# One transpose and one product per differential step, four buffers for squares, and convolution taps turned by TensorE

## What is computed

```python
# differential attention: two softmax maps of one head, subtracted
sc = einsum('bqhcd,bkhcd->bchqk', qb, k) * scale + bias
p = softmax(where(dist >= 0, sc, -inf), axis=-1)
w = p[:, 0] - lam * p[:, 1]
out = einsum('bhqk,bkhd->bqhd', w, v)          # then rmsnorm over each head's 128 values

# feed-forward: a causal convolution of three taps per channel, then a gate
u = causal_dwconv(h @ ffn_up, ffn_conv_w, ffn_conv_b)
u_gate, u_val = split(u, 2)
x = x + (gelu(u_gate) * u_val) @ ffn_down

# SSD mixer: chunk by chunk, at its end a norm over each group of 512 channels
return grouped_rms_norm(y * silu(z), norm_w, SSD_GROUPS)
```

## Time and profile before

| | |
|---|---|
| median of 3 runs | 3296.1 us (3293.46 to 3296.81) |
| the profiled execution's own time | 3299.9 us |
| its span, first to last instruction | 3298.2 us |
| TensorE matmuls busy | 3095.4 us, 94% |
| VectorE, ScalarE, GpSimd busy | 43%, 34%, 23% |
| mean granted TensorE clock | 0.972 of full speed |

### The profile page before, as it was taken

One profiled execution on the slowest core, in us unless ns is written; L12 is line 12 of the kernel. 1 busy time (PEld: TensorE's weight loads), 2 busy tenths in 40 slices (PEclk: granted clock), 3 DMA queues, 4 the chain that ended last, 5 costly groups with the idle time before them and its releaser, 6 DMA issues. The chain is left out here.

```text
span 3298.2 us, 39762 instructions
## 1 busy us (share of the span) xinstructions
PE 3095.4 (94%) x15115; PEld 2529.9 (77%) x15115; DVE 1422.1 (43%) x2254; ACT 1120.1 (34%) x1462; POOL 746.5 (23%) x482
## 2 busy tenths in 40 slices
PE   8998899989999999989999999978798999999988
PEld 6676777777877788868888888857777888878766
DVE  4345223411134522334434343464533556546666
ACT  4344233412136622223222222242332445324333
POOL 2000100012222122212114321202422333123333
PEclk9999999999999999989999999989899999899979
DMA  3110111022221222341111111125033110322223
GB/s 131 41 33 7 46 51 30 1 48 66 60 62 43 68 64 64 109 62 51 45 38 58 51 45 38 45 76 96 10 105 103 44 34 26 109 44 68 81 78 121
DMA packets 275520, 194.10 MB, mean 59 GB/s; under 512 B 66617, under 2 KB 246969, under 8 KB 275393
## 3 DMA queue, kind: packets, MB, share of 16 engines
q1 hardware_dynamic: 273280, 191.33, 20.6%
q10 hardware_dynamic: 2112, 1.05, 0.1%
HBM read 165.77 MB, written 26.57 MB: 58 GB/s over the span
## 5 line engine op out<-in xcount | busy, mean ns | idle before, releaser
L138 POOL TENSOR_TENSOR w_low<-w_raw,w_high 128x1024 fp32r<-128x1024 f32 (+1 forms) x180 | 416.0, 2311 | 1802.2 <-ACT w_high L131 1799.0
L156 PE MATMUL ffn_banks<-act_high,w_high 128*128 128x512 f32 x704 | 276.7, 393 | 12.2 <-POOL w_low L138 8.2
L131 ACT ACTIVATE w_high<-w_raw 128x1024 fp32r<-128x1024 f32 (+1 forms) x180 | 179.3, 997 | 313.6 <-PE mix_banks L156 173.4
L156 PE MATMUL ffn_banks<-act_low,w_high 128*128 128x512 f32 x704 | 276.3, 392 | 0.0
L156 PE MATMUL ffn_banks<-act_high,w_low 128*128 128x512 f32 x704 | 276.0, 392 | 0.0
L156 PE MATMUL mix_banks<-act_high,w_high 128*128 128x512 f32 x640 | 254.1, 397 | 10.3 <-ACTq L609 6.0
L156 PE MATMUL mix_banks<-act_high,w_low 128*128 128x512 f32 x640 | 249.9, 390 | 0.0
L156 PE MATMUL mix_banks<-act_low,w_high 128*128 128x512 f32 x640 | 249.8, 390 | 0.0
L156 PEld LDWEIGHTS ffn_banks<-act_high,w_high 128*128 128x128 f32 x704 | 133.7, 190 | 41.2 <-POOL w_low L138 8.8
L1736 PE MATMUL ffn_banks<-v_high,f_high 128*128 128x512 f32 x352 | 142.3, 404 | 15.2 <-issue 8.3
L156 PEld LDWEIGHTS ffn_banks<-act_high,w_low 128*128 128x128 f32 x704 | 133.6, 190 | 28.0
(11 more groups left out here) (640 smaller groups left out, 7216.1 us busy)
## 6 DMA issues: line engine op xcount, KB each, us to landing
w_raw<-in_w_in SPq DMA_DIRECT2D x106, 512.0 KB, 4.1
w_raw<-in_ffn_up SPq DMA_DIRECT2D x44, 512.0 KB, 3.8
w_raw<-in_w_out SPq DMA_DIRECT2D x24, 512.0 KB, 4.3
v_raw<-in_ffn_down SPq DMA_DIRECT2D x11, 1024.0 KB, 5.0
decay<-acum_rows SPq DMA_DIRECT2D x16, 512.0 KB, 3.7
x_ring<-in_x SPq DMA_DIRECT2D x8, 512.0 KB, 10.4
m_part<-gate SPq DMA_DIRECT2D x8, 512.0 KB
other<-m_part SPq DMA_DIRECT2D x8, 512.0 KB, 3.7
```

What stands on the lines that cost most here:

```text
L131: act.activation(self.high[slot][:, 0:nk, :], self.raw[slot][:, 0:nk, :], ACT.Copy).then_inc(self.s("high", slot), 1)
L138: pool.tensor_tensor(self.low[slot][:, 0:nk, :], self.raw[slot][:, 0:nk, :], self.high[slot][:, 0:nk, :].bitcast(F32), ALU.subtract).then_ ...
L156: last = pe.matmul(out[:, h, :] if not halves else out[h], w[slot][:, k, :], x[:, k, cols], start=(n == 0), stop=(n == 3 * nk - 1))
```

## The change

Four edits, and nothing else of the program's order:

1. In the differential attention, VectorE forms one map out of two (`combine`): map 0 plus map 1 times the ratio of the row sums times minus lambda. Only this map is transposed, copied and multiplied by V; `take` divides by the first row sum. `combine(j+1)` stands in VectorE's list behind `reduce(j+2)`, and ahead of `scale_out` and `take(j)`.
2. In SSD, the four squares have a buffer each, and `sums_early` moves from the end of round 10 into round 11, behind `diagonal`. `rstd(0)` and the root go to round 11 as well.
3. In the feed-forward part, taps, biases and two of S5's vectors come as rows of 512 bytes, TensorE transposes them (three transposes, between the first two projections), and ScalarE copies them out. The first turn's tiles now stand ahead of `c_rows` and `b` in SP's list.
4. In the gated mix, ScalarE frees the banks before it waits for `gate_b`.

```diff
@@ gated mix, ScalarE
-                act.wait_ge(sem("gate_b"), 48)
                 for j in two:
                     act.sem_inc(sem(f"pg_free{j}"), 1)
+                act.wait_ge(sem("gate_b"), 48)
@@ stage_attention
+    sides = range(1 if diff else 2)
+    NS = len(sides)
-    groups = [(i, c, g, min(4, b + 1 - g)) for i, b in enumerate(order) for c in range(2) for g in range(0, b + 1, 4)]
+    groups = [(i, c, g, min(4, b + 1 - g)) for i, b in enumerate(order) for c in sides for g in range(0, b + 1, 4)]
...
-                        pe.wait_ge(sem("probs"), 2 * j + c + 1)
+                        if diff:
+                            pe.wait_ge(sem("combined"), j + 1)
+                        else:
+                            pe.wait_ge(sem("probs"), 2 * j + c + 1)
...
+                def combine(j):
...
+                    dve.wait_ge(sem("probs"), 2 * j + 2)
+                    dve.reciprocal(part[:, b, :], total[:, b, :]).then_inc(sem("part"), 1)
+                    dve.wait_ge(sem("part"), j + 1)
+                    dve.scalar_tensor_tensor(out=ratio[:, b:b + 1], in0=total[:, b, 0:1], scalar=signs[:, 1:2], in1=part[:, b, 1:2],
+                                             op0=ALU.mult, op1=ALU.mult).then_inc(sem("ratio"), 1)
+                    dve.wait_ge(sem("ratio"), j + 1)
+                    dve.scalar_tensor_tensor(out=S[j % 2][:, 0, 0:n], in0=S[j % 2][:, 1, 0:n], scalar=ratio[:, b:b + 1], in1=S[j % 2][:, 0, 0:n],
+                                             op0=ALU.mult, op1=ALU.add).then_inc(sem("combined"), 1)
...
                     if j + 2 <= last_step:
                         reduce(j + 2)
+                    if diff and j < last_step:
+                        combine(j + 1)
@@ stage_ffn, SyncE and TensorE
-                S5.load_c(sp)
                 turn(0)
+                S5.load_c(sp)
                 S5.load(sp)
...
                 project(0, 0, 0)
+                turn_rows()
                 project(0, 0, 1)
@@ SSD, TensorE and ScalarE
+                    if it == NB + 3:
+                        sums_early()
...
-                    if it == NB + 2:
-                        sums_early()
...
-                    if 2 <= k < 4:
-                        act.wait_ge(sem("summed"), k - 1)
-                    elif k == 4:
+                    if k == 4:
                         act.wait_ge(sem("summed"), 4)
...
-                    out = total if k == 4 else sq[k % 2]
+                    out = sq_early[k] if k < 4 else total if k == 4 else sq[k % 2]
```

More of the change, by code:

```diff
@@ L1158, in stage_attention @@
         part = sbuf(core, ctx, "part", [P, NB, 2])
+        ratio = sbuf(core, ctx, "ratio", [P, NB]) if diff else None
         mask = sbuf(core, ctx, "mask", [P, P])
@@ L1297, in turned @@
                             pe.wait_ge(sem("ev_dve"), dves_to(N - 1))
-                        if i == 1 and h and n < ends[0, 1] + 2:
+                        if i == 1 and h and n < ends[0, NS - 1] + 2:
                             pe.wait_ge(sem("yl"), 2 * (h - 1) + n % 2 + 1)
@@ L1306, in values @@
                     b = order[i]
-                    for c in range(2):
+                    for c in sides:
                         pe.wait_ge(sem("ev_act"), acts_to(h * GN + ends[i, c]))
@@ L1546, in _ @@
                 reduce(1)
+                if diff:
+                    combine(0)
                 evacuate(0)
@@ L1602, in stage_ffn @@
         UG, UV = lay.take("u_gate", [P, SEQ]), lay.take("u_val", [P, SEQ])
-        taps = lay.take("taps", [P, 3, 2 * FCH])
-        bias = lay.take("bias", [P, 2 * FCH])
+        conv = lay.take("conv", [P, 4, 2 * FCH])
+        taps, bias = conv[:, 0:3, :], conv[:, 3, :]
+        conv_rows = [lay.take(f"conv_rows{j}", [4 * FCH, P]) for j in two]
+        lam_rows = lay.take("lam_rows", [2 * S5_PAIRS, P])
+        log_step = lay.take("log_step", [P, 2 * S5_PAIRS])
         lay = Overlay(core, T.rest.at, T.rest.end - T.rest.at)
@@ L1637, in _ @@
             def _(sp):
-                for j in range(3):
-                    sp.dma_start(taps[:, j, :], per_channel(io["ffn_conv_w"][0, j])).then_inc(sem("small"), 16)
-                sp.dma_start(bias[:, :], per_channel(io["ffn_conv_b"][0])).then_inc(sem("small"), 16)
+                for j in range(4):
+                    vector = io["ffn_conv_w"][0, j] if j < 3 else io["ffn_conv_b"][0]
+                    sp.dma_start(conv_rows[j // 2][j % 2 * 2 * FCH:(j % 2 + 1) * 2 * FCH, :], vector.rearrange("(k p) -> k p", p=P)).then_inc(sem("small"), 16)
+                S5.load_rows(sp, lam_rows, log_step)
                 def turn(i):
```

71 lines of the change are left out of this document (45 added, 26 removed).

## The result

The changed kernel takes 3238.56 us (median of 4 runs, 3235.09 to 3241.29) against 3294.78 us, a ratio of 0.9828 with a 95% interval of 0.9811 to 0.9845: 1.7% faster, 56 us. The forecast was 3241. (The kernel before now has a fourth run, which moves its median from 3296.1 to 3294.78 us.)

The account below looks back on a forecast made before the run. TensorE, busy 94% of the span, was taken as the bound. Edits 1, 4, 3 and 2 summed as -36.6 - 3.5 - 10.6 - 4.1 = -54.8 us, from 3296.1 to 3241 us, range 3224 to 3262.

Parts of the forecast that it names:

- Edit 1, -36.6 forecast: Differential attention: -38.8 in 22 steps, -5 in the last ten, +2 start, +0.2 later openings, +2 clock, +3 GpSimd.
- The covered steps: Differential attention, first 22 of 32 steps: projection matmuls keep TensorE the bound; 56.4 x 22/32 = -38.8 us.
- The cover is just long enough: Differential attention, first 22 steps: VectorE's path of 3.4 us fits TensorE's 3.0 to 3.7 us of other work.
- The last head: Differential attention without projections: chain of scores, sums, combine, transposes, 36.5 us less some 2; gains 3 us.
- The clock, +2 forecast: Differential attention openings: last pause grows from 2.40 to about 4 us; clock stays low longer or falls elsewhere, +2 us.
- Edit 2, -4.1 forecast: SSD: sums start 0.9 us later, `turn_y` follows at once, -6.1; slow transposes and output products, +2; bounds -1 and -9.
- Edit 3, -10.6 forecast: Feed-forward: two tile waits -8.2, two slow periods -4.4, new transposes +0.6, a later wait +1.4 us.
- What is late next: Feed-forward: VectorE's 5.5 us of S5 angles meets the first output products, which then wait about 1.4 us.
- GpSimd's hold: Rival, differential attention: each of eight splits stops a combine, up to 19 us instead of 3; 3257 us, chance 0.11.
- VectorE's pace: Rival, differential attention: 0.7 us more per step, 15 us back, plus 7 us of slower clock; 3263 us, chance 0.09.
- given back by the small edits: Rival, edits 2, 3 and 4: another wait follows each pause, 12 of 18 us go; 3253 us, chance 0.12.
- the slowest rival: Rival, differential attention: pauses at head openings leave TensorE's clock at 0.50, slower than before; above 3303 us, chance 0.03.

Follow-up runs that it names:

- the last kernel of the study: Changed kernel with slot 1's split behind the opening, scores ahead of transposes in the last ten steps, eight projection matmuls ahead at openings; 3227.27 us, ratio 0.9784.
- the narrow combine: Changed kernel with the combine's wide operation cut to 2 columns, leaving out the sum of the two maps elsewhere; 3229.53 us, ratio 0.9792.
- their four ratios: Kernel before with one of the four edits each, in order: 0.9881, 0.9980, 0.9977, 0.9992; 3258.44, 3291.32, 3290.43, 3295.30 us.

## Why the prediction was right, point by point

**Edit 1, -36.6 forecast, -37.0 to -38.8 measured.** The covered steps came as worked out. Values and transposes gave 31.8 and 20.2 us where 31.3 and 18.0 had been forecast; a head's period fell by 13.0 us, 1.63 us a step, against 56.4/32 = 1.76 less the openings. "The cover is just long enough" holds, with something to spare: the wait of 0.5 us once a head stands behind a hold of 1.38 us, so in that step there was room for some 0.9 us more (an estimate, their difference). With the combine behind `take` it no longer sufficed in any of the first head's steps. The wide combine took the 1.28 us taken from the earlier trace rows.

Two terms were off, and partly cancel. The last head was to gain 3 us and gained 6.8 (from opening to opening 44.4 us before, 37.6 after). From its first wide transposes to its last values the chain took 31.4 us (283.23 to 314.61), and I had 34.5, the 36.5 us of a whole head less 2 that the head before does. That 2 was too small: when these transposes began, scores and sums of three of the eight steps, 11 of 36 blocks, and two combines were done. By my own terms this is 9.5 us, and would leave 27; the other 4.4 us of the chain my sum lacked, and what they are is open. And the third head, with its two bare steps and the last opening, fell by 8.1 us, 4.9 less than a covered head; by my sum it would have been 1.5 less (2 x 1.76 less 2). Of the difference, 2 us are GpSimd's hold on `scale_out`. I had asked which combines it would hold and priced that at 3 us; it held the `ratio` of four of them, 0.5 us of waiting in each of three heads, and the scaling, 1.9 us: some 3.4 us in this stage. That size is in part luck, as the 0.08 us at the other openings show.

**The clock, +2 forecast.** Right in kind. It was 0.77 for 6 us behind the covered openings, where in the kernel before it hadn't fallen (1.00 from 190 to 196 us), and the last kernel of the study shows the price, 0.8 us on the transposes and some more on what follows. At every covered opening with one pause of 2.54 us (this kernel and four others) the clock fell to between 0.72 and 0.78 over 6 us; with two shorter ones (before, the narrow combine, the last kernel) it stayed at 1.00. The pause at the last opening was 5.08 us and not 4.

**Edit 2, -4.1 forecast, -6.6 measured,** inside its bounds. The mis-sized term is the sums. I had states and diagonal slow for 5 us, so that the sums start 0.9 us later, at 0.216 us each. That step didn't follow from its own numbers, since 5 us of work fit into a wait of 6.46. They started where they had (236.7 and 236.8 us after the stage's first matmul), and the first half ran faster (TensorE, kernel after, and two windows):

```profile
3093.40 5.23 PE L2486 MATMUL ssd_banks<-ones,sq 128*128 128x1 f32 x32 [1.17 <-ACT sq L2590]
...
3105.80 1.12 PE L2458 MATMUL ssd_banks<-ident,y 128*128 128x128 f32 x4 [0.34 <-DVE y L2733]
...
3093.00:3098.00 5.00, 4.56 (x30) 4.48 (x31) 2.57 (x2) 5.00 (x6) 0.00 (x0) 0.78 0.35 105
3098.00:3103.00 5.00, 5.00 (x25) 5.00 (x25) 3.90 (x4) 4.98 (x6) 1.63 (x1) 0.50 0.01 3
```

With states and diagonal ahead of them in place of a pause, the clock was higher at the start of the sums, and fell back to 0.50 under the one-column products. `turn_y` came 8.3 us sooner, and the slow start of the output products gave 1.7 back, where I had 2.

**Edit 3, -10.6 forecast, -8.9 measured.** No wait is left at the second and third tile, and the clock is 1.00 from 1386 to 1448 (next to last row of the fence): the 8.2 and 4.4 us are there. "What is late next" was named rightly, S5's angles on VectorE ahead of the first output products, but priced at 1.4 us. It is 2.96 us. GpSimd again (VectorE, GpSimd, the window and TensorE, kernel after):

```profile
1441.99 0.31 DVE L3686 TENSOR_TENSOR powers<-count,values 128x144 f32<-128x144 f32 x1
1442.34 2.43 DVE L3687 TENSOR_TENSOR powers<-powers 128x144 f32<-128x144 f32 x1
...
1442.21 2.40 POOL L138 TENSOR_TENSOR w_low<-w_raw,w_high 128x1024 fp32r<-128x1024 f32 x1 [8.47 <-ACT w_high L131]
...
1386.00:1448.00 62.00, 59.48 (x267) 48.77 (x265) 27.60 (x41) 21.77 (x24) 16.64 (x6) 1.00 0.40 106
...
1448.45 0.50 PE L1772 MATMUL ffn_banks<-v_high,f_high 128*128 128x512 f32 x1 [2.96 <-DVE x L1952]
```

An operation of the same kind and size as the one ahead of it, 0.31 us, took 2.43, until the split that had begun 0.13 us before it was over. The run with edit 3 alone has the same 2.43 and 2.96 us. These 2.1 us are more than the 1.7 by which the edit was off. That the rows, and not the order, carry this edit the prediction didn't separate.

**Edit 4, -3.5 forecast,** 2.8 us on the wait and 0.3 behind it. I had read the starts of other stages as 1.2 to 2.7 us. In the profile before the five starts without `gate_b` are 2.7 to 7.3 us (2.68, 3.07, 4.05, 4.90, 7.32), and this one is now 3.16.

**The rivals.** GpSimd's hold was the right mechanism, mostly at other instructions than the wide combine: on the path some 3.4 us in the attention, and 2.1 us on a product of S5. VectorE's pace is excluded by the narrow combine. Nothing was given back by the small edits, as their four ratios show. The clock cost 2.8 us at the two covered openings, by the last kernel (1.4 in each head behind one), where 2 had been allowed for; and it came back each time (1.00 from 296 to 310), so the slowest rival is out. That the total came within 3 us of the forecast is in part cancelling: edits 1 and 2 gave 2.2 and 2.5 us more than forecast, edits 3 and 4 gave 1.7 and 0.5 less. Not settled is the rest, the 7.5 us by which the profiled executions differ in untouched stages. The distance of the two executions from their medians, 8.6 us in all, covers it; but the 2 us of the stretch behind the S5 mixer go with the kernel and not with the execution, so some of it may be in the medians.

## What to carry to other kernels

Work that is taken off the bounding engine is worth its time only if what replaces it is done before that engine comes to ask for it: count the cover, step by step, between the two places in the lists. One place further back in VectorE's list made the stage 38 us longer here. And a change of order that shortens one wait has to be followed to whoever waits for what was pushed back, as `c_rows` showed.

## What was not expected of the hardware

- A hold by GpSimd lasts until GpSimd's operation is over, whatever is held, so a small instruction loses as much as a large one: 1.9 us were added to a scaling of 1024 columns (3.13 us, 1.22 without it), 2.1 to a product of 144 columns (2.43), 1.6 to a square of 128 (1.87, which reads one tensor twice) and 1.4 to 1.9 to a `ratio` of one column. It matters where the held instruction stands, not how long it is.
- A shorter pause of TensorE needn't be followed by a shorter slow period. The pause went from 5.08 to 3.17 us, and the stage was no shorter, with the clock at 0.56 and 0.78 in two windows of 12 us where it had been 0.54 and 0.89. But one pause of 2.54 us split in two of 1.62 and 0.95 left the clock at 1.00 where it had been 0.72. And behind waits of 1.49 and 0.69 us the same code was at 0.72 in one execution and at 1.00 in another.
- The clock was at 0.50 under sums over one column: TensorE was busy with them for all of the 5 us from 3098 to 3103, behind 5 us at 0.78. Before the change they ran at 0.50 for 13.5 us.
